# Layer 0's gate products taken tile by tile, turned probabilities copied on ScalarE, and layer 1's shift summed wholly on VectorE

## The reference

```python
def adaln(c, w, b):                                   # w is 2048 x 6144, once per layer
    m = jax.nn.silu(c) @ w + b
    shift, scale, gate = jnp.split(m, 3, axis=-1)
# per layer, for prompt (c_ctx) and latent tokens (c):
h = rmsnorm(x, norms[i]) * (1.0 + scale) + shift
# layer 0: q_a k_a v_a q_b k_b v_b gate = split(h @ w_in);  A: 8 query heads on 2 key heads,
#          B: 8 heads with a bias and a window; both softmax attention, own keys plus context keys
# layer 1: latent attention with 16 heads from q_lat, kv_lat, k_rope, gate = split(h @ w_in)
out = (o * jax.nn.silu(gate)) @ w_out
x = x + gate_ada * out
```

## Time and profile before

| | before |
|---|---|
| median of 3 runs | 1343.76 us |
| the profiled execution | 1343.44 us, span 1341.4 us |
| TensorE busy | 97% of the span, granted clock 0.998 |
| VectorE, ScalarE busy | 59%, 36% |
| DMA | 257.8 MB, mean 192 GB/s |

### The profile page before, as it was taken

The page is one execution under the profiler, slowest core; times in us unless marked ns, Lnnn a source line. Parts: engine busy times, 40 slices in busy tenths (PEclk is TensorE's granted clock), DMA queues, the critical chain, the costliest instruction groups (busy, mean ns, idle before and its releaser), DMA issues.

```text
span 1341.4 us, 17064 instructions
## 1 busy us (share of the span) xinstructions
PE 1304.5 (97%) x6643; PEld 1029.3 (77%) x6643; DVE 794.2 (59%) x1180; ACT 489.1 (36%) x816; POOL 62.5 (5%) x80
## 2 busy tenths in 40 slices
PE   5999999999999999999999899999999999999997
PEld 2567777877778778878887688887788888878885
DVE  3334775886677658656785566885454444453445
ACT  4324332342223322343334653333353433433333
POOL 2000100000100020001000200000000000001000
PEclk9999999999999999999999999999999999999999
DMA  9999787645886247533775467574331112216443
GB/s 377 389 402 397 244 315 250 209 151 185 294 290 206 92 142 247 192 95 110 286 257 172 142 210 227 199 223 135 114 99 59 64 64 63 61 52 240 152 150 133
DMA packets 70111, 257.80 MB, mean 192 GB/s; under 512 B 8504, under 2 KB 8632, under 8 KB 68752
## 3 DMA queue, kind: packets, MB, share of 16 engines
q1 hardware_dynamic: 64368, 235.48, 51.1%
q0 software_dynamic: 5520, 21.17, 4.8%
q10 hardware_dynamic: 144, 0.07, 0.0%
HBM read 248.76 MB, written 7.93 MB: 191 GB/s over the span
## 4 chain that ended last, share of the span: by engine, by line
PE 74%; DVE 4%; issue 2%; ACT 1%; POOL 0%; DVEq 0%; ACTq 0%; POOLq 0%
PE gemm L507 16%; PE gemm L509 16%; PE gemm L508 16%; PE attended L701 3%; PE turned L651 3%; PE gemm L479 2%; PE gemm L481 2%; PE gemm L480 2%; PE scores L946 2%; PE scores L950 1%; PE scores L687 1%; PE ada_bank L481 1%; PE ada_bank L480 1%; PE ada_bank L479 1%; DVE w_lo L1389 1%
## 5 line engine op out<-in xcount | busy, mean ns | idle before, releaser
L1389 DVE TENSOR_TENSOR w_lo<-w_raw,w_hi 128x1024 fp32r<-128x1024 f32 x242 | 297.5, 1232 | 280.0 <-ACT w_hi L1023 279.2
L507 PE MATMUL gemm<-w_hi,act_lo 128*128 128x512 f32 x1146 | 458.2, 400 | 0.4 <-DVE w_lo L1389 0.4
L509 PE MATMUL gemm<-w_hi,act_hi 128*128 128x512 f32 x1146 | 447.3, 390 | 0.0
L508 PE MATMUL gemm<-w_lo,act_hi 128*128 128x512 f32 x1146 | 446.7, 390 | 0.0
L1023 ACT ACTIVATE w_hi<-w_raw 128x1024 fp32r<-128x1024 f32 x242 | 253.9, 1056 | 369.8 <-PE gemm L509 323.4
L507 PEld LDWEIGHTS gemm<-w_hi,act_lo 128*128 128x128 f32 x1146 | 215.3, 188 | 55.8 <-issue 13.4
L509 PEld LDWEIGHTS gemm<-w_hi,act_hi 128*128 128x128 f32 x1146 | 215.1, 188 | 46.3
L508 PEld LDWEIGHTS gemm<-w_lo,act_hi 128*128 128x128 f32 x1146 | 215.5, 188 | 42.2
L1079 ACT ACTIVATE prob<-scores,nmax 128x384 f32<-128x384 f32 (+1 forms) x96 | 48.9, 510 | 173.2 <-DVE nmax L1578 161.7
L1584 DVE COPY probT<-turned 128x384 f32<-128x384 f32 (+1 forms) x96 | 44.7, 466 | 74.1 <-PE turned L651 73.7
L1578 DVE TENSOR_REDUCE nmax<-scores 128x1 f32<-128x384 f32 (+1 forms) x96 | 42.5, 464 | 52.8 <-PE scores L950 48.6
(11 more groups left out here) (303 smaller groups left out, 1541.9 us busy)
## 6 DMA issues: line engine op xcount, KB each, us to landing
w_raw<-in_w_all SPq DMA_DIRECT2D x245, 512.0 KB, 3.7
ada<-in_ada_all SPq DMA_DIRECT2D x168, 512.0 KB, 7.0
gate_ring<-in_ada_all SPq DMA_DIRECT2D x24, 512.0 KB, 4.2
gate_bc<-gate_scratch POOLq DMA_DIRECT2D x4, 1024.0 KB, 7.2
st<-x_scratch POOLq DMA_DIRECT2D x4, 768.0 KB, 5.1
x_scratch<-u POOLq DMA_DIRECT2D x3, 768.0 KB, 4.3
u<-in_x_sample SPq DMA_DIRECT2D x2, 1024.0 KB, 8.3
bias<-in_bias_all POOLq DMA_DIRECT2D x2, 1024.0 KB, 7.9
```

The source lines that it names most:

```text
L507: pe.matmul(bank_[:], alo, whi[:, kk], start=first, stop=False)
L508: pe.matmul(bank_[:], ahi, wlo[:, kk], start=False, stop=False)
L509: last = pe.matmul(bank_[:], ahi, whi[:, kk], start=False, stop=end)
L1389: dve.tensor_tensor(w_lo[:, r, 0:width], w_raw[:, r, 0:width], hi_slot(w)[:, 0:width].bitcast(F32), ALU.subtract).then_inc(lo_ready, 1)
```

## The change

1. **Unit stages of A0, A1, B0.** The next chunk's 24 tile products stand two by two in the twelve units, instead of eight whole slots in eight units.
2. **ScalarE copies.** In layer 0's unit stages the copy of the turned probabilities moves from VectorE to ScalarE, ahead of the exponent of n + 2; in B0 and B1 so do the copies of the turned queries and keys. ScalarE's gate evacuation moves inside unit 0.
3. **Layer 1's shift wholly as running sums.** Third 3's two visits go; its 8 transfers go through `v_ring` and become 8 products of two instructions. The running sums get accumulators of their own: `rows`/`u`, two pairs in the ring slots that the visits no longer use, and `rows`/`late_acc`, which now lies over `swapped` and the rotary tables.
4. **Placement.** Third 5's two visits move from B0 to A1 (after its slots 3 and 5). Four products more stand in B0's units 2 to 9 and four in B1's slots 18, 19, 20 and 22.
5. **Layer 1's first pair.** One product ahead of its first unit, the other behind its first attention.

TensorE, group B0, the units 3 and 4: first before, then with the change. `gemm` rows are slot matmuls, `attended` x3 is a wide attention.

The core of the diff:

```diff
-SUMS = [(4, 0, 0), (4, 1, 0), (3, 0, SHARED), (3, 1, SHARED)]
+SUMS = [(4, 0), (4, 1), (3, 0), (3, 1)]
...
-        late_acc = sb("late_acc", [P, 2, 2, CH], F32, at=bias_at)
-        sums_of = [[rows[:, 0:2, :], u[:, 0:2, D - CH:D]]] * 3 + [[late_acc[:, 0], late_acc[:, 1]]]
+        late_acc = sb("late_acc", [P, 2, CH], F32, at=late_at)
+        halves = ada.rearrange("p r (g n) -> p r g n", g=2)
+        sums_of = [[rows[:, 0:2, :], u[:, 0:2, D - CH:D]], [halves[:, 0], halves[:, 1]],
+                   [halves[:, 2], halves[:, 3]], [rows[:, 0:2, :], late_acc[:]]]
...
-        P_THIRDS = [(2, KT), (3, SHARED), (5, SHARED)]
+        P_THIRDS = [(2, KT), (5, SHARED)]
         visits = {W_A + 2 * q + 1: (0, q) for q in range(SPC)}
-        for n in range(2):
-            for q in range(SHARED // 2):
-                visits[W_B + 9 * n + 3 + 3 * q] = (1 + n, q)
+        for q in range(SHARED // 2):
+            visits[W_A + 2 * SPC + 3 + 2 * q] = (1, q)
...
+        sums_in_units = {n: 2 * KT + (n - 2) // 2 for n in range(2, 10)}
...
@@ TensorE, group A (B0 in the same way)
+                    for piece in (2 * n, 2 * n + 1):
+                        j = piece // NT
+                        chunk_slot((W_A + SPC + j + i * (2 * SPC)), j, m + NT, tiles=[piece % NT])
                     for j in beside(n):
-                        chunk_slot((W_A + SPC + j + i * (2 * SPC)), j, m + NT)
                         ada_visit(W_A + SPC + j + i * (2 * SPC))
...
@@ TensorE, layer 1's pairs
                     if alone:
-                        for c in range(2):
-                            pair_product(following, c)
+                        pair_product(following, 0)
...
-                    elif not alone:
+                    else:
                         pair_product(following, n + 1)
...
@@ ScalarE, a group's unit stage
-                evacuate_gate(m, (W_A + SPC - 1 + i * (2 * SPC)), i * CH, [0, 1])
-                exponent(n0 + 2, 2)
-                evacuate_gate(m, (W_A + SPC - 1 + i * (2 * SPC)), i * CH, [2])
                 for n in range(UNITS):
-                    if 2 < n + 2 < UNITS:
+                    if n == 0:
+                        evacuate_gate(m, (W_A + SPC - 1 + i * (2 * SPC)), i * CH, [0, 1])
+                    prob_copy(n0 + n, n % NT, tau + (1 + GROUP + n))
+                    if n + 2 < UNITS:
                         exponent(n0 + (n + 2), (n + 2) % NT)
+                    if n == 0:
+                        evacuate_gate(m, (W_A + SPC - 1 + i * (2 * SPC)), i * CH, [2])
...
@@ ScalarE, group B's slots
+                    if 2 <= j < 6:
+                        copy_turned(tau + (j - 2), qT[:, j - 2, :], TOK)
+                    if SPC + 2 <= j < SPC + 6:
+                        h = j - SPC - 2
+                        copy_turned(tau + (GROUP + h), kT[:, h, :], KEYS, SC0)
```

More of the change, by code:

```diff
@@ L232, in build @@
         krows = sb("krows", [P, 4, 2, ROPE], at=bias_at + (2 * CH + KEYS) * 4)
+        late_at = top[0]
         swapped = sb("swapped", [P, CH])
@@ L430, in load_sum @@
                 need(sp, v_used, v + 1 - V_RING)
-                part = [n for n in range(len(SUMS)) if v >= sum_first[n]][-1]
-                third, half, k0 = SUMS[part]
-                at = third * HALVES + 2 * (k0 + v - sum_first[part]) + half
+                third, half = SUMS[v // KT]
+                at = third * HALVES + 2 * (v % KT) + half
                 sp.dma_start(v_ring[:, v % V_RING, :], t_in["ada_all"][at]).then_inc(v_in[v % V_RING], 16)
@@ L452, in _ @@
                     load_visit(*visits[in_order[in_order.index(slot) + 1]])
-                for v in range(V_RING, sum_first[-1]):
+                for v in range(V_RING, V_END):
                     if sums_at[v - V_RING] == slot:
@@ L826, in _ @@
                     else:
-                        for j in beside(n):
-                            chunk_slot((w0 + 3 * SPC + j), j, m + (3 * NT))
+                        for piece in (2 * n, 2 * n + 1):
+                            j = piece // NT
+                            chunk_slot((w0 + 3 * SPC + j), j, m + (3 * NT), tiles=[piece % NT])
                 attend_b(UNITS - 1)
@@ L1081, in exponent, with copy_turned, prob_copy @@
                                accum_out=rsum[:, n % 4:n % 4 + 1]).then_inc(p_ready, 1)
+            def copy_turned(tau, out, cols, scale=1.0):
+                need(act, t_done, tau + 1)
+                copy(out, TB[:, 0:cols], scale).then_inc(t_free, 1)
+            def prob_copy(n, t, tau):
+                need(act, pv_done, n - 1)
+                width = P if t == 0 else 3 * P
+                copy_turned(tau, probT[:, n % 2, 0:width], width)
             def square_sums(rows_, sizes, at, width, before):
@@ L1190, in _ @@
                 if i == N_B - 1:
[L1191 to L1194, removed]
+                    act.wait_ge(rows_free, ROWS_0 + 3)
+                w_gate = w
                 for n in range(UNITS):
-                    if 2 < n + 2 < UNITS:
+                    if n == 0:
+                        evacuate_gate(m + (2 * NT), w_gate, i * CH + N_A * CH, [0, 1])
+                    prob_copy(n0 + n, n % NT, tau + (2 * GROUP + n))
+                    if n + 2 < UNITS:
                         exponent(n0 + (n + 2), (n + 2) % NT)
+                    if n == 0:
+                        evacuate_gate(m + (2 * NT), w_gate, i * CH + N_A * CH, [2])
                     for j in beside(n) if i < N_B - 1 else []:
@@ L1464, in add_part @@
             def add_part(part):
-                third, half, _ = SUMS[part]
+                third, half = SUMS[part]
                 add_sums(third, slice(64 * half, 64 * half + 64), AD, part + 1)
@@ L1477, in part_product @@
             def part_product(at, v):
-                part = [n for n in range(len(SUMS)) if at >= sum_first[n]][-1]
-                first = at == sum_first[part]
+                part, k = at // KT, at % KT
                 slot = v_ring[:, at % V_RING, :].rearrange("p (g n) -> p g n", g=2)
@@ L1484, in part_product @@
                     need(dve, v_used, at)
-                    if first:
-                        need(dve, summed, part)
-                last = add_product(sums_of[part][v], slot, SUMS[part][2] + at - sum_first[part], v, first)
+                    if part == 3 and k == 0:
+                        need(dve, t_done, T_B + T_B_PER + 2 * GROUP)
+                last = add_product(sums_of[part][v], slot, k, v, k == 0)
                 if v == 1:
@@ L1763, in _ @@
                     part_product(i * SPC + 2 + n // 2, n % 2)
+                    if i == 1 and n == 4:
+                        add_rows(5, P_END)
                 output(n0 + (UNITS - 1), NT - 1, i * CH + (GROUP - 1) * P)
@@ L1803, in _ @@
                         split_lo(W_B + (i * 4 + 3) * SPC + j + 2)
+                    if i == 0 and n in sums_in_units:
+                        part_product(sums_in_units[n], n % 2)
                     if i == N_B - 1 and n % NT == 2:
@@ L2091, in gate_rows @@
                 pool.wait_ge(*after)
-                pool.wait_ge(rows_free, ROWS_0 + 4 + 4 * layer)
+                pool.wait_ge(rows_free, ROWS_0 + 5 + 2 * layer)
                 for v in range(2):
```

46 lines of the change are left out of this document (18 added, 28 removed).

## The result

The changed kernel takes 1331.05 us (median of 4 runs, 1330.37 to 1331.28). The kernel before took 1343.78 us on the same chip. The ratio is 0.9905 with an interval of 0.9888 to 0.9922. The change gained 12.7 us.

A forecast was written before the change was run, and what follows sets the result against it. The prediction took TensorE, busy 97% of the span, as the bound. Visits −3.9, B1's start +0.7, waits −6.4 and cutting +1.1 summed to −8.5 us, giving 1335.3 us against the median, range 1332.8 to 1340.6.

The forecast's parts named there:

- The waits that go: Seven `attended` waits in A0, A1, B0 go, 4.3 us; with query, key, B1 and layer 1 pair waits, −6.4 us.
- C: Three unit stages and B1: the 12 changes and B1's start cost nothing, 1333.5 us, or 1333.4 with B1's rest; 6%.
- The finer cutting: A0, A1, B0: 12 more changes between attention and gemm, about 0.09 us each, +1.1 us; bounds 0 and +2.
- B1's start: First units of B1: maxima 1.1 us late and copies queued on ScalarE delay TensorE, +0.7 us; bounds 0 and +2.
- The visits: TensorE, layer 1's shift: two visits fewer at 1.95 us each, −3.9 us, with nothing covering them.
- The copies: Layer 0's units, copies moved to ScalarE: cost 0; without cover, `turned` waits at most 0.3 to 0.5 us per unit.
- Outside layer 0: No growing waits counted outside layer 0; layer 1's first pair loses its 0.9 us wait for an exponent.
- rival D: Three unit stages: finer cutting brings TensorE's lower clock for a tenth of the units, +15 us, some 1350; 2%.
- A: Unit stages: waits stay in part, `turned` waiting for ScalarE's copies; four fifths of 6.4 us stay, 1340.4 us; 14%.
- B: B1 and B0: VectorE's added 20.4 us of products come late in its fixed list, delaying TensorE; 1346 us, 8%.

The follow-up runs named there:

- the cutting alone: The kernel before, with only layer 0's gate products cut into tiles, two per unit: 1337.51 us, ratio 0.9955.
- the sums alone: The kernel before, with only the change's running sums, visits and placement; whole slots, copies on VectorE, first pair as before: 1339.94 us, ratio 0.9972.
- The doubled changes: The changed kernel, with each unit's two tiles apart, so TensorE changes between attention and gemm 36 times more: 1334.28 us, ratio 0.9931.
- copies alone: The kernel before, with only layer 0's copies of turned probabilities, queries and keys (B) on ScalarE: 1343.37 us, ratio 0.9998.
- the kernel without gate visits: The changed kernel, with third 5 wholly as running sums, both A1 visits gone, eight more products on VectorE: 1329.56 us, ratio 0.9894.
- one visit fewer: The changed kernel, with one more visit of third 5 gone and four more products among layer 1's gate sums: 1328.28 us, ratio 0.9885.

## Why the prediction was wrong in size and right in kind

**The waits that go: right in which, mis-sized by 2.8 us.** This is the step that failed. I took seven waits at the 4.3 us that the profile shows. By starts there were nine, three in each of the three stages. B0's longest is shown as 1.17, but scores at 447.46 and attention at 449.02 are 1.56 apart, where 0.23 is the distance without a wait: 1.33. The gemm behind it then comes 0.22 after the attention instead of 0.14. That is about 0.24 beyond what is shown, which I take for each of the seven. Two waits, one in A0 and one in A1, are not shown at all. The timeline of TensorE before, in A0:

```profile
208.97 0.39 PE L687 MATMUL scores<-kT,qT 128*128 128x128 f32 x2
209.41 0.46 PE L701 MATMUL attended<-kT,probT 128*128 128x128 f32 x2
209.62 0.48 PE L507 MATMUL gemm<-w_hi,act_lo 128*128 128x512 f32 x1
```

and the same matmuls after, at a unit of B0:

```profile
442.22 0.39 PE L691 MATMUL scores<-kT,qT 128*128 128x128 f32 x2
442.45 0.39 PE L705 MATMUL attended<-v,probT 128*128 128x128 f32 x2
442.59 0.48 PE L511 MATMUL gemm<-w_hi,act_lo 128*128 128x512 f32 x1
```

Before, 0.44 and 0.21 us between starts; after, 0.23 and 0.14. That is 0.28 us lost with nothing shown, since the scores' row ends at 209.36 and only 0.05 us before the attention is left, too little for the view to print. So 4.3 + 7 x 0.24 + 2 x 0.28 = 6.5 us; the cutting alone measured 1.65 + 1.72 + 2.91 = 6.3, with the cost of the cutting in it. The other waits were short in the same way: the pair's 0.9 gained 1.26, A1's query wait of 0.6 about 0.7 (A1 in the sums alone: 2 x 2.06 − 3.43). B1 gained 0.73, where I had 0.6. In all 9.2 us, not 6.4. The missing 2.8 us alone put the sum at 1332.5, under the range: its lower end stood 0.6 us under C, and C too had the waits at 6.5 at the most. The Trainium skill (Perfetto Trace Analysis, its note ahead of the first section) warns of matmul busy time "because matmuls are pipelined". By the rows above the same holds of the idle time beside it here, and the front of this document says that a matmul's cost is read from starts. I kept to that for the visits and not for the waits.

**The finer cutting: 0.02 us per change, not 0.09.** I had charged the longer first gemm distance (0.31 instead of 0.23) and not credited what falls away when attention no longer stands against attention: from a wide attention to the next turned block it was 0.66 us (446.47 to 447.13 before), and to a gemm matmul it is 0.59 (446.38 to 446.97 after). The doubled changes give 0.2 us for 12. So +0.2 instead of +1.1, which is rival C's assumption.

**B1's start: 0 instead of +0.7.** The products in the slots 18 to 22 made the maxima late by less than I took, and there was slack behind them. The first maximum before, and its scores on TensorE:

```profile
590.79 1.03 PE L687 MATMUL scores<-kT,qT 128*128 128x128 f32 x4
591.26 0.29 DVE L1578 TENSOR_REDUCE nmax<-scores 128x1 f32<-128x128 f32 x1 [1.64 <-PE scores L687]
```

and after, with the first copy on ScalarE and the next turned block:

```profile
577.03 1.22 DVE L1416 TENSOR_TENSOR w_lo<-w_raw,w_hi 128x1024 fp32r<-128x1024 f32 x1 [0.30 <-ACT w_hi L1029]
578.18 1.28 DVE L1501 SCALAR_TENSOR_TENSOR rows<-ada,silu_c,rows 128x1024 f32<-128x1024 f32 x1
579.37 1.28 DVE L1501 SCALAR_TENSOR_TENSOR late_acc<-ada,silu_c,late_acc 128x1024 f32<-128x1024 f32 x1
579.42 1.03 PE L691 MATMUL scores<-kT,qT 128*128 128x128 f32 x4
580.57 0.28 DVE L1604 TENSOR_REDUCE nmax<-scores 128x1 f32<-128x128 f32 x1
...
585.25 0.31 ACT L1029 ACTIVATE probT<-turned 128x128 f32<-128x128 f32 x1
...
586.55 0.49 PE L655 MATMUL turned<-ident,prob 128*128 128x128 f32 x3
```

The product of slot 22 is over at 580.65, and the first maximum comes 1.15 us after its scores instead of 0.47: 0.7 us later than before, not 1.1. But the first copy ends at 585.56, 1.0 us before TensorE's next turned block, where I had it 0.5 us too late. No `turned` waits for an exponent or a copy in B1. The table bears it out: copies alone and the whole change both have −0.73 there.

**The visits: right.** Two fewer are 4.1 us, not 3.9. B0 without four of them gained 8.09 (sums alone) to 8.24 (11.15 less the 2.91 of the cutting), so up to 2.06 each; I had left out the slower start behind a visit (turned block to gemm 0.30 us at 342.77, against 0.24 at 495.09, both before). The other figure that I had weighed, 0.9 us for a visit by the Trainium skill's 216 ns (TensorE: Matmul & The Clock Gate, Back-to-back issue gap) and side-by-side groups, is not borne out.

**The copies: right that they cost nothing, wrong that they do little.** Alone they are worth nothing measurable. With the new sums they keep a wait for a query out of B1 (+1.11 turns into −0.73). I had looked at how many products VectorE gets, and not at what each one meets.

**Outside layer 0: right.** No wait grew there, nothing but the first pair moved, and the clock stayed; the groups of 12 gemm matmuls between attentions did not lower it, so rival D falls. A falls too, as no copy is waited for. B fell here and is shown real by the kernel without gate visits.

The sum again, with the measured sizes: −4.1 (visits) − 9.2 (waits) + 0.2 (cutting) = −13.1, and +0.3 at the start, which the change does not touch: −12.8, where the span fell by 12.9.

## What to carry to other kernels

Price a TensorE wait by the distance between the starts on either side, less the distance the same pair has where nothing waits; "idle before" leaves out the tail of the last matmul (here 0.16 to 0.24 us per wait) and hides short waits wholly. Where an in-order engine waits between pairs of small steps, spread the filler evenly over all of them (here twelve places of 12 matmuls instead of eight of 18): the finer cut cost 0.02 us a place and gave back 6.3 us. When work moves from a full engine to one that waits often, move it until a wait appears at a named slot, and then go back one step: by starts one visit fewer gained 2.0 us more, and of that two fewer gave back 0.5.

## What the runs showed of the hardware

**A long wait cost twice.** One wait of 4.6 us brought TensorE to its lower level for some 7 us (granted 0.52, then 0.67) and cost about 2.9 us on top. It is one event in one profiled execution. None of the thirteen waits of at most 2.8 us did.

**VectorE's products and weights stood still while GpSimd added; a copy out of PSUM did not.** In the kernel before, a `TENSOR_SCALAR` of 128x1024 took 5.10 us instead of 0.75, beside a GpSimd add of 5.18. VectorE's timeline, and GpSimd's:

```profile
497.58 5.10 DVE L1473 TENSOR_SCALAR rows<-ada,silu_c 128x1024 f32<-128x1024 f32 x1
```

```profile
496.94 5.18 POOL L2082 TENSOR_TENSOR bias<-bias,mask 128x2048 f32<-128x2048 f32 x1 [7.48 <-DMA bias<-in_bias_all]
```

VectorE began 0.6 us after GpSimd and ended 0.6 us after it. Beside B0's add in the same kernel, the copy of a turned query took its usual 0.56 us, and the `w_lo` behind it 3.65 instead of 1.23:

```profile
336.90 0.56 DVE L1584 COPY qT<-turned 128x384 f32<-128x384 f32 x1 [1.07 <-PE turned L651]
337.73 3.65 DVE L1389 TENSOR_TENSOR w_lo<-w_raw,w_hi 128x1024 fp32r<-128x1024 f32 x1 [0.27 <-ACT w_hi L1023]
```

```profile
335.26 5.03 POOL L2082 TENSOR_TENSOR bias<-bias,mask 128x2048 f32<-128x2048 f32 x1 [7.39 <-DMA bias<-in_bias_all]
```

The Trainium skill (SBUF — State Buffer, SBUF: two separate sides) has the two engines share one pair of ports as an exclusive lock, held for the whole instruction, where VectorE's instruction runs in a 2-port perf mode or has two SBUF inputs. The trace agrees for the `w_lo`, which has two such inputs, and for the copy, which has none. The `TENSOR_SCALAR` has one tensor input, and no row shows in which mode it runs. TensorE did not wait in either place. With the sums alone it did, by 1.11 us. So a product should not stand on VectorE where GpSimd's add falls if a copy that TensorE waits for stands behind it.
